# Token differences of a Strassen-style projection placed behind the weight splits, and an earlier first split for the down projection

## The reference

```
x = x + 1/2 (1+g1) * SwiGLU_1(mod1(rmsnorm(x)))
x = x +     (1+g2) * Mix(mod2(rmsnorm(x)))
x = x + 1/2 (1+g3) * SwiGLU_2(mod3(rmsnorm(x)))
out = rmsnorm(x)
SwiGLU(h) = (silu(h @ w1) * (h @ w3)) @ w2        w1, w3: 1024 x 2816, w2: 2816 x 1024
```

## Time and profile before

| | us |
|---|---|
| median of 3 runs (lowest, highest) | 1124.14 (1123.91, 1127.47) |
| the profiled execution | 1124.16 |
| its span in the trace | 1122.4 |
| PE busy | 1101.6 |
| DVE busy | 643.9 |
| ACT busy | 562.0 |

### The profile page before, as it was taken

One profiled execution on the slowest core, in us unless ns is written; L12 is line 12 of the kernel. 1 busy time (PEld: TensorE's weight loads), 2 busy tenths in 40 slices (PEclk: granted clock), 3 DMA queues, 4 the chain that ended last, 5 costly groups with the idle time before them and its releaser, 6 DMA issues.

```text
span 1122.4 us, 16847 instructions
## 1 busy us (share of the span) xinstructions
PE 1101.6 (98%) x6110; PEld 927.8 (83%) x6110; DVE 643.9 (57%) x1068; ACT 562.0 (50%) x1006; POOL 197.9 (18%) x123
## 2 busy tenths in 40 slices
PE   7999999999999999999999999999899999999998
PEld 5678888888888888877778888887699999978887
DVE  4544454545343485569986637677677777742232
ACT  4564646465445344245657654444655555522233
POOL 0055454545333321030101000040000000000000
PEclk9999999999999999999999999999999999999999
DMA  9856655566776628359999913324376666553222
GB/s 325 277 159 197 220 172 169 191 221 194 262 254 229 198 76 254 113 142 245 209 208 198 199 57 97 93 75 169 95 221 182 183 182 182 171 176 102 83 71 76
DMA packets 241106, 194.44 MB, mean 173 GB/s; under 512 B 5671, under 2 KB 238754, under 8 KB 240802
## 3 DMA queue, kind: packets, MB, share of 16 engines
q1 hardware_dynamic: 179760, 127.68, 38.0%
q10 hardware_dynamic: 44786, 47.25, 12.9%
q0 software_dynamic: 16512, 18.87, 10.3%
HBM read 189.59 MB, written 41.94 MB: 206 GB/s over the span
## 4 chain that ended last, share of the span: by engine, by line
PE 91%; ACT 3%; DVE 3%; DMA 1%; issue 1%; SPq 0%; ACTq 0%; DVEq 0%
PE ps L432 22%; PE ps L434 22%; PE ps L433 22%; PE ps L691 5%; PE ps L693 5%; PE ps L692 5%; PE ps L1856 2%; PE ps L1834 1%; PE ps L1821 1%; DVE w_lo L411 1%; DMA ada<-in_w_ada 1%; ACT w_hi L406 1%; PE ps L1801 1%; PE ps L1628 1%; PE ps L999 1%
## 5 line engine op out<-in xcount | busy, mean ns | idle before, releaser
L411 DVE TENSOR_TENSOR w_lo<-raw,w_hi 128x1024 fp32r<-128x1024 f32 (+1 forms) x128 | 194.6, 1522 | 268.6 <-ACT w_hi L406 268.3
L432 PE MATMUL ps<-h_hi,w_hi 128*128 128x512 f32 x720 | 287.2, 399 | 7.6 <-DVE w_lo L411 5.3
L406 ACT ACTIVATE w_hi<-raw 128x1024 fp32r<-128x1024 f32 (+1 forms) x128 | 145.5, 1138 | 278.2 <-PE ps L434 269.4
L434 PE MATMUL ps<-h_hi,w_lo 128*128 128x512 f32 x720 | 281.5, 391 | 0.0
L433 PE MATMUL ps<-h_lo,w_hi 128*128 128x512 f32 x720 | 281.2, 391 | 0.0
L432 PEld LDWEIGHTS ps<-h_hi,w_hi 128*128 128x128 f32 x720 | 135.6, 188 | 43.8 <-DVE w_lo L411 7.5
L434 PEld LDWEIGHTS ps<-h_hi,w_lo 128*128 128x128 f32 x720 | 135.5, 188 | 29.1
L433 PEld LDWEIGHTS ps<-h_lo,w_hi 128*128 128x128 f32 x720 | 135.8, 189 | 26.3 <-issue 0.2
L432 PE MATMUL ps<-g_hi,w_hi 128*128 128x512 f32 x330 | 129.9, 394 | 2.1 <-DVE w_lo L411 2.0
L434 PE MATMUL ps<-g_hi,w_lo 128*128 128x512 f32 x330 | 128.6, 390 | 0.0
L433 PE MATMUL ps<-g_lo,w_hi 128*128 128x512 f32 x330 | 128.5, 389 | 0.0
(11 more groups left out here) (307 smaller groups left out, 1835.7 us busy)
## 6 DMA issues: line engine op xcount, KB each, us to landing
ada<-in_w_ada ACTq DMA_DIRECT2D x27, 1024.0 KB, 5.1
raw<-in_w_ffn SPq DMA_DIRECT2D x24, 1024.0 KB, 5.5
raw<-in_w_ffn SPq DMA_DIRECT2D x16, 1408.0 KB, 6.9
w_s<-in_w_ffn ACTq DMA_DIRECT2D x8, 2304.0 KB, 14.3
s_raw<-w_s SPq DMA_DIRECT2D x72, 256.0 KB, 3.1
raw<-in_w_in SPq DMA_DIRECT2D x64, 256.0 KB, 8.9
w_s<-in_w_ffn POOLq DMA_DIRECT2D x4, 2304.0 KB, 38.6
w_s<-w_s POOLq DMA_DIRECT2D x4, 2304.0 KB, 33.5
```

What stands on the lines that cost most here:

```text
L406: nc.scalar.activation(tiles_of(w_hi[j % SPL], nk), raw_of(f, j, nk), ACT.Copy).then_inc(hi_done, 1)
L411: nc.vector.tensor_tensor(tiles_of(w_lo[j % SPL], nk), raw_of(f, j, nk), tiles_of(w_hi[j % SPL], nk).bitcast(F32), ALU.subtract).then_inc( ...
L432: nc.tensor.matmul(ps[:, bank, :], hi, rhs_hi, start=start, stop=False)
L434: return nc.tensor.matmul(ps[:, bank, :], lo, rhs_hi, start=False, stop=stop)
```

## The change

Place 1, around units 112 to 115 and the first set. The shifts, differences and splits of the token differences, which stood between the pairs, now stand behind pair (1,0) on both ACT and DVE. The half that is shifted first is now nrm (half 1), then u_a (half 0). The second difference is made before the third. The split of the third difference stands behind the block splits a, s1, s2, and the fourth difference too.

Place 2, in the last set. The split of unit 116's weights moves up on both engines: on ACT from behind the last corner to ahead of it, on DVE from behind the last set to ahead of `dve_glo` in it.

```diff
@@ token_diff
+            if t == 2:
+                dve.wait_ge(shifted, BL)
+                dve.wait_ge(t_step, 1)
+                nc.vector.tensor_tensor(t2, nrm[:, :, HS:SEQ], t1, ALU.add).then_inc(t_step, 1)
             if t == 3:
                 dve.wait_ge(shifted, 2 * BL)
                 nc.vector.tensor_tensor(t3, u_a[:, :, HS:SEQ], nrm[:, :, HS:SEQ], ALU.subtract).then_inc(t_step, 1)
-            if t == 2:
-                nc.vector.tensor_tensor(t2, nrm[:, :, HS:SEQ], t1, ALU.add).then_inc(t_step, 1)
             if t == 4:
-                dve.wait_ge(t_step, 3)
+                dve.wait_ge(t_step, 2)
@@ token_hi
-            act.wait_ge(t_step, (1, 3, 2, 4)[t - 1])
+            act.wait_ge(t_step, t)
@@ act_set
+            if last_set(q, m):
+                act.wait_ge(prod_done, number("s2", q, m))
+                hi_u(act, U_DOWN[1])
             act_corner(act, q, m)
@@ dve_set
+            if last_set(q, m):
+                lo_u(dve, U_DOWN[1])
             if m == 1 and not second_set(q, m):
                 dve_glo(dve, q - 1)
@@ act_up2
             act_pair(act, 1, 0, 0, KD)
+            act_pair(act, 1, 0, 1, KD)
+            act_pair(act, 1, 1, 0, KD)
+            token_shift(act, 1)
             token_shift(act, 0)
-            act_pair(act, 1, 0, 1, KD)
             token_hi(act, 1)
-            token_shift(act, 1)
-            act_pair(act, 1, 1, 0, KD)
             token_hi(act, 2)
+            act_pair_silu(act, 1, 1)
+            for name in ("a", "s1", "s2"):
+                block_hi(act, name, 0, 0)
             token_hi(act, 3)
-            act_pair_silu(act, 1, 1)
-            for name in ("a", "s1", "s2", "d"):
-                block_hi(act, name, 0, 0)
+            block_hi(act, "d", 0, 0)
             act_first_product(act, 0, 0)
             token_hi(act, 4)
...
             sets(act, act_set)
-            act.wait_ge(prod_done, number("s2", QUADS - 1, 1))
-            hi_u(act, U_DOWN[1])
@@ dve_up2
             dve_pair(dve, 1, 0, 0, KD)
+            dve_pair(dve, 1, 0, 1, KD)
+            dve_pair(dve, 1, 1, 0, KD)
             token_diff(dve, 1)
-            dve_pair(dve, 1, 0, 1, KD)
+            token_diff(dve, 2)
             token_lo(dve, 1)
-            dve_pair(dve, 1, 1, 0, KD)
             token_diff(dve, 3)
-            token_diff(dve, 2)
-            token_diff(dve, 4)
             token_lo(dve, 2)
-            token_lo(dve, 3)
             for name in ("a", "s1", "s2"):
                 block_lo(dve, name, 0, 0)
+            token_diff(dve, 4)
+            token_lo(dve, 3)
             dve_pair_g(dve, 1, 1)
             block_lo(dve, "d", 0, 0)
             token_lo(dve, 4)
...
             sets(dve, dve_set)
-            lo_u(dve, U_DOWN[1])
```

## The result

The changed kernel takes 1119.39 us in the median of 6 runs (1118.69 to 1120.22), the kernel before 1125.01 in the median of 6 (1123.91 to 1127.47). The ratio is 0.9943, 95% interval 0.9932 to 0.9954: faster by 6.4 us, 5.2 to 7.7. The two medians lie 5.6 us apart and the means of the six runs each 5.9; 0.9943 is what comes out when the 13 runs of the kernel before that were timed next are taken in, whose median is 1126.51. Forecast were 1119.1 us and a gain of 5.0. The time was met; the gain is somewhat larger than the sum, and the experiments show where the rest is likely to lie.

The account below looks back on a forecast made before the run. PE, busy 1101.6 of 1122.4 us, bounds the kernel, so only its waits can be won. Gains of 3.5 us (place 1) and 1.5 us (place 2) take 1124.16 to 1119.1 us, range 1117.3 to 1121.2.

Parts of the forecast that it names:

- the sum: Whole kernel: 3.5 us at place 1 plus 1.5 us at place 2, 5.0 us off 1124.16, giving 1119.1 us.
- The splits at place 1: Ahead of unit 114: weight splits end near 786.9, PE does not stop, and unit 115 ends 7.1 us earlier.
- What is late next: First set: token work behind pair (1,0) delays d to 807.10, with PE waits of 2.0 and 1.5 us; gain 3.5 us.
- So DVE's list, not PE, sets the start of d in both kernels: First set: h_lo ended at 810.56, just before d at 810.65, so DVE's list was taken to set d before and after.
- The clock: At place 1's new waits of 2.0 and 1.5 us: no fall of the granted clock, costed at nothing.
- rival B: At place 1: the pair of waits lowers the clock as d resumes, costing 1.6 us; gain 3.4, 1120.8 us; chance 0.08.
- my one row: Trace row of the kernel before: a wait of 2.1 us at place 2 left the granted clock at 1.00.
- Place 2: Last set: unit 116 starts 2.1 us sooner, a new 0.7 us wait precedes the late product; gain 1.5 us.
- the forecast's own range: Whole kernel: 1117.6 to 1120.5 us, before widening to take in rival outcomes; chance of the forecast 0.79.

Follow-up runs that it names:

- idle slots filled: Against the changed kernel: nrm shifts and first difference moved between the weight splits of units 114 and 115; 1117.18 us, ratio to the kernel before 0.9919.
- u_a first: Against the changed kernel: u_a shifts, then the first token split, then nrm shifts, behind pair (1,0); 1121.37 us in a single run.
- place 1 alone: Against the changed kernel: unit 116's weight split put back behind the last set on both engines; 1122.4 us, ratio to the kernel before 0.9966.
- dve_glo first: Against the changed kernel: in the last set `dve_glo` stays ahead of w_lo of unit 116 on DVE; 1118.48 us, ratio to the kernel before 0.9932.
- place 2 alone: Against the kernel before: only unit 116's weight split moved up on both engines; 1123.72 us, ratio 0.9978.
- second look: The kernel before, unchanged, traced once more to see how much its trace varies; 1127.16 us in 1 run.

## Why the prediction was right

- **The splits at place 1** went as worked out: w_lo of 114 began at 785.75 and was done by 787, no wait ahead of unit 114, 7.1 us sooner at product a's turn.
- **What is late next**: the step on which the forecast depends, that the token work behind the pair holds d and gives back half of the 7.1 us, was right to 0.1 us (h_lo 807.18 for 807.04). The kernels with the idle slots filled and with u_a first move h_lo by 2.6 and 2.1 us and d goes along. That d itself came when forecast is in part a near tie: behind a_lo PE took 5.87 us from a to d at the lower clock, and DVE 5.82 from the end of a_lo to that of h_lo.
- **"So DVE's list, not PE, sets the start of d in both kernels"** is wrong for the kernel before. There PE set it: d followed s2 without a pause, and h_lo itself hung on PE, by way of the copy of product a on ACT. The gain is unchanged, since d started at 810.65 either way, but whoever had kept PE busy in the old kernel would have won 1.5 us that this sentence says are not there.
- **The clock** was costed at nothing because one wait of 2.1 us had left it up. It fell in the changed kernel behind such a wait. This step was wrong, and that the time was met all the same is luck: the fall came ahead of a, where the 1.5 us that PE would have waited for d took it up; rival B had put it at d. The section of the Trainium skill that has the clock fall back behind brief idle spells that come often ("TensorE: Matmul & The Clock Gate", "A second HAM failure mode: psum-queue depth-cycling") pointed in the right direction where my one row did not. The traces go beyond it: a single wait of 2 us was enough in six of seven cases.
- **Place 2** was right in each part: no wait ahead of unit 116, `dve_glo` behind w_lo, 0.6 us of PE ahead of the late product, 1.5 us gained of 2.1.
- **The size**: 5.0 for 4.7 in the traces. The 6.4 us of the timed runs probably hold in addition what the kernel before loses at its long waits in most of its executions. A slip of the sum: 1.2 us later than 1119.1 is 1120.3, where the forecast's own range has 1120.5; nothing hangs on it.

## What to carry to other kernels

When a wait is removed, walk the list of the engine behind it to the next meeting point and compute when that is ready: here half of the gain was spent there, and the idle slots on the same two lists (2.9 us on ACT and 2.8 on DVE, in sight in the timeline) gave 2.6 us back without new work. An instruction that is moved up takes its place in a strict list: ask what it passes; 0.75 us came back by letting a short ready instruction stay ahead of one that waits for a load. And a gain beside a wait of a few us should be read from more than one trace of the kernel before.

## What the runs showed of the hardware

The granted clock behind a wait of PE of about 2 us is not settled by its length. At place 2 a wait of 1.96 or 1.97 us left it at 1.00 in one trace and was followed by the 1.2 GHz level in three. Ahead of the first set a wait of 2.08 us was followed by it in all three traces that have it (changed, place 1 alone, dve_glo first: from a to d 5.87 us in each, for three products that take 4.31 at the full clock). Behind waits of 0.5 to 1.2 us it stayed up in each trace. In the wait of 5.3 us at place 1 it fell in all three traces that have it (both looks at the kernel before and place 2 alone), in the last two while PE still stood (second look: 0.52 from 792 to 794, PE busy for 0.00 us). Matmuls of no use in the gap kept it at 1.00, in one trace each for 2.2 us and for 5.1 us, and cost no time that could be seen, since PE had to wait.
